# Two transformer layers on one core: index heads in pairs, a wide first block with x split ahead of w, and a norm chunk divided over two groups

## The chip, the cores and the metric

The kernel runs on one core of one Trainium2 chip. Its time is the device time of one execution in microseconds; the median over several executions is given. Engines are named as in the profile: TensorE (PE, with its weight loads as PEld), VectorE (DVE), ScalarE (ACT), GpSimd (POOL) and SyncE (SP), which issues most of the DMAs.

## What is computed

Two layers run one after the other over x of 256 tokens by 2048 (float32). The first layer is a mixer of two attentions, a cross attention to a memory, and a feed-forward part, each followed by a layer norm. The part in which the change lies is the start of the mixer:

```python
proj = x @ w_in
q_dsa, c_kv, q_idx, k_idx, w_idx, q_m, k_m, v_m, ga, gb = split(proj)
c_kv = rms_norm(c_kv, kv_norm_g)
k_idx = layer_norm(k_idx, idx_k_norm_g, idx_k_norm_b)
...
logits = einsum('thd,sd->ths', q_idx, k_idx) * 64 ** -0.5       # 16 index heads of 64
score = einsum('th,ths->ts', w_idx * 16 ** -0.5, relu(logits))  # summed over the heads
score = where(key_pos <= qpos, score, -inf)                     # then the top 64 keys of each query
...
x = layer_norm(ALPHA * x + y, ln_g[0], ln_b[0])                 # the first norm, ahead of the cross attention
```

The second layer (a gated mixer of three attention branches) is not touched.

## The kernel before

**Blocks and groups.** Every projection is cut into blocks of 512 output columns (`NB`), one accumulation for each of the two token tiles (`R = 2`). The contraction over 2048 rows is cut into 16 tiles of 128, taken two at a time (`GK = 2`): one block is 8 groups, and a group is 12 matmuls of 128 x 128 by 512. Twelve, because float32 operands are split into an upper part in the fast format and a rest (x = x_hi + x_lo, w = w_hi + w_lo), and the products hi*hi, hi*lo and lo*hi are summed.

**How a group of weights comes.** SP loads it into one of four slots of `stage` (`group`, L277; it waits until VectorE has finished the group four back, semaphore `lo_done`). ScalarE rounds it to `w_hi` (`split`, L1031, L1043), VectorE subtracts to get `w_lo` (`split`, L1446, L1454), and TensorE's `group` (L542) waits for `lo_done` and multiplies (L552). ScalarE and VectorE run two groups ahead of TensorE (`AHEAD = 2`): their `weights` functions call `split` twice at the first group of a block, once at each of the others but the last, and not at the last. Other work of a stage is put between the groups by hooks: `hook(j)` runs behind group j on every engine. Each engine works through its own list strictly in order.

**The start.** `x` comes in four chunks of 512 columns (`x_chunk`, L297) over SP's queue, the first piece of weights over ScalarE's (L1129). TensorE runs filling turns (`keep_warm`), then turns x by 128 x 128 tiles (`feed_batch`, L590, L594), two batches ahead; ScalarE writes `x_hi` of a batch (`hi_batch`, L1085) and VectorE `x_lo` (`lo_batch`, L1495). Block 1 holds the 256 columns of c_kv and the 80 of k_idx and w_idx (`FIRST_W = 336`), loaded as two pieces per group (256 columns, then 80), and VectorE copies its result out (L1649 to L1656). On ScalarE and VectorE the split of w group 0 stands ahead of the first batch of x. Blocks 2 and 3 are q_idx (512 columns each), 4 and 5 q_dsa, 6 to 9 q and k of the second attention ("qk_m"), 10 and 11 its values. ScalarE copies each of these blocks to `nat` (`to_nat`), TensorE turns it behind group 0 of the next block (`turn`, L571, L577), VectorE copies the turned heads (`heads_in`). The small norms of k_idx and c_kv run on VectorE in the hooks of block 2 (`small_norms`), their results are turned behind group 2 of block 4 (`keys_and_latent`).

**Index heads.** In each of the blocks 6 to 9, behind groups 0, 2, 4 and 6, one of the 16 heads is scored (`index_head`, TensorE L704, ScalarE L1158, VectorE L1717). TensorE multiplies two tiles of queries (128 columns of keys for the first, 256 for the second) into the PSUM bank `AUX`; the head takes 64 of the 128 rows of the array, the lower and the upper half by turns. ScalarE writes the relu to `relu_s`, VectorE adds it, weighted, to `score`. POOL copies the eight tiles of q_idx for the next block after the fourth head.

**The first norm.** The residual is kept in `x_res` (two tiles of 2048 columns). After the last output block, in the block that projects the memory's keys ("K block", weights `w_kv_mem`), VectorE computes the root of the variance behind group 0 (`norm_root`, L1618, which also does the first 256 columns), the next 256 columns behind group 1 (`norm_chunk(0)`) and the 512 columns of the second chunk behind group 2 (`norm_chunk(1)`): `centre` (L1605) and `rescale` (L1614), two instructions each. POOL does the two last chunks at the same time (L494, L500, L505). TensorE turns the finished columns behind groups 5 and 6 and in the next block ("Q block").

```python
            def norm_in(j):

                if j == 0:
                    norm_root(64)
                if 1 <= j <= 2:
                    norm_chunk(j - 1)
                feed_into(x_hi, x_lo, FED_X[0])(j)
```

Of the kernel before, what the change touches and what calls it, by code (L numbers as in the profile page):

```python
# [28 lines left out]
P = 128  # L29
# [115 lines left out]
def two_blocks(nc, a, out, per):  # L145

    ctx = ExitStack()
    with ctx:
# [118 lines left out]
        def width(g):  # L267

            return NB if not isinstance(g, int) or g >= KT // GK else FIRST_W
# [3 lines left out]
        def _(sp):  # L273
# [30 lines left out]
            group(a["w_in"], GK * P, C_LAT, FIRST_W)  # L304
            x_chunk(1)
            group(a["w_in"], 2 * GK * P, C_LAT, FIRST_W)
            group(a["w_in"], 3 * GK * P, C_LAT, FIRST_W)
# [229 lines left out]
        def _(pe):  # L537
# [3 lines left out]

            def group(kt, first, last, hi, lo, n=NB):  # L542
# [17 lines left out]
            def weights(kts=KT, hi=x_hi, lo=x_lo, n=NB, hook=None, before=None):  # L560
                groups = kts // GK
                for j in range(groups):
                    if before:
                        before(j)
                    group(j * GK, j == 0, j == groups - 1, hi, lo, n)
# [114 lines left out]
            feed_weights(x_in, x_landed, n=FIRST_W, warm=lambda: keep_warm(3))  # L680
# [346 lines left out]
        def _(act):  # L1027
# [3 lines left out]
            def split():  # L1031
# [5 lines left out]
                parts = 2 if isinstance(g, int) and (g < KT // GK or G_UV <= g < G_UV + H_DSA * HD // NB) else 1  # L1037
# [91 lines left out]
            for at, width_, to in ((C_LAT, LAT, 0), (C_KIDX, KIDX_W, LAT)):  # L1129
                src = a["w_in"][0:GK * P, ds(at, width_)].rearrange("(t p) n -> p t n", p=P)  # L1130
                act.dma_start(stage[:, 0, :, to:to + width_], src).then_inc(sem("landed0"), 16)
# [16 lines left out]
            for b in range(2):  # L1148
                weights(hook=small_roots if b == 0 else None)
                to_nat()  # L1150
                c.next("tp_done", 2)
            c.next("tp_done", 2)
# [289 lines left out]
        def _(dve):  # L1442
# [198 lines left out]
            split()  # L1641
            for t in range(KT // 2):
                lo_batch(x_hi[:, 2 * t:2 * t + 2, :], x_lo[:, 2 * t:2 * t + 2, :], t)
                if t > 0:
                    split()
                c.next("w_used")
            split()

            for r in range(R):  # L1649
# [7 lines left out]
            split()  # L1657
# [58 lines left out]
            dve.wait_ge(sem("ext"), 32)  # L1716
            def index_head(b, j):  # L1717

                if j % 2:
                    return  # L1720
                dve.wait_ge(sem("idx_read"), c.next("idx_read"))
                for t, (lo, hi) in enumerate(TILE_COLS):
                    ins = dve.scalar_tensor_tensor(
                        out=score[:, lo:hi], in0=relu_s[:, lo:hi],
                        scalar=flat(w_idx[:, t:t + 1, b * 4 + j // 2:b * 4 + j // 2 + 1]),
                        in1=score[:, lo:hi], op0=ALU.mult, op1=ALU.add)
                ins.then_inc(sem("relu_used"), 1)
                dve.wait_ge(sem("relu_used"), c.next("relu_used"))
# [9 lines left out]
            def heads_of(b):  # L1738

                dst, b = (qi_t, b) if b < 2 else (qd_t, b - 2) if b < 4 else (qkm_t, b - 4)  # L1740
                heads_in(lambda t: dst[:, b * 4 + 2 * t:b * 4 + 2 * t + 2, :])

            for b in range(8):
                def q_hook(j):
                    if b > 0 and j == 0:
# [3 lines left out]
                    if b == 0:  # L1749
# [3 lines left out]
                    if b >= 4:  # L1753
                        if j == 0 and b == 4:
                            dve.wait_ge(sem("const"), 1)
                        index_head(b - 4, j)
# [104 lines left out]
            def norm_in(j):  # L1861
# [3 lines left out]
                if 1 <= j <= 2:  # L1865
                    norm_chunk(j - 1)
# [327 lines left out]
```

## Time and profile before

| | us |
|---|---|
| median of 3 runs (lowest, highest) | 2265.49 (2264.25, 2270.46) |
| profiled execution | 2264.81 |
| span in its profile, mean granted clock | 2263.0, 0.996 |
| TensorE busy, instructions | 2240.2, 10253 |
| weight loads (PEld) busy | 1853.4 |
| VectorE busy | 1307.0 |
| ScalarE busy | 1039.1 |
| GpSimd busy | 171.3 |
| DMA: moved, mean rate | 421.28 MB, 186 GB/s |

Matmuls are pipelined: one row of a 512-column matmul shows about 390 ns, while the next one starts 227 ns after it. So rows of the timeline overlap, and the distance between starts is what a matmul costs. In the rows below, "Lnnn" is the line of the kernel; "x12" merges twelve instructions that follow each other.

### The profile page before, as it was taken

The numbers are of one execution on the slowest core, as the hardware profiler recorded it, in microseconds if no ns is written. First come the engines' busy times: TensorE is split into PE (matmuls) and PEld (weight loads), VectorE is DVE, ScalarE is ACT, GpSimd is POOL, SyncE is SP. The second block draws the span as 40 slices with busy tenths as digits, with TensorE's granted clock in tenths as the row PEclk, the third lists the DMA queues.
The fourth block names the chain that finished last, engine by engine and source line by source line (L and its number), as shares of the span: only waits on it lengthen the run. The fifth ranks groups of instructions, "written<-read, shape, count | busy, mean of one in ns | idle before, by whom it ended". The sixth has DMA issues, their size and how long they took to land.

```text
span 2263.0 us, 29600 instructions
## 1 busy us (share of the span) xinstructions
PE 2240.2 (99%) x10253; PEld 1853.4 (82%) x10253; DVE 1307.0 (58%) x1571; ACT 1039.1 (46%) x1239; POOL 171.3 (8%) x175
## 2 busy tenths in 40 slices
PE   8999999999999999999999999999999999999999
PEld 7877888888887788888888888887888888888887
DVE  5555655666667764455445544567565656645674
ACT  4444444555444444433444344435545454445642
POOL 1000000001204130000000000004000000200020
PEclk9999999999999999999999999999999999999999
DMA  7755554656755466656565566554556665665554
GB/s 220 227 166 155 175 163 155 195 154 216 253 187 204 131 206 193 189 192 192 179 200 187 194 190 194 186 186 149 167 176 202 194 195 176 214 186 175 168 190 163
DMA packets 216437, 421.28 MB, mean 186 GB/s; under 512 B 15224, under 2 KB 19360, under 8 KB 214432
## 3 DMA queue, kind: packets, MB, share of 16 engines
q1 hardware_dynamic: 212640, 401.97, 56.7%
q0 software_dynamic: 3168, 17.82, 2.4%
q8 instruction: 55, 0.90, 0.2%
q10 hardware_dynamic: 544, 0.34, 0.1%
q14 instruction: 30, 0.25, 0.0%
HBM read 417.97 MB, written 2.11 MB: 186 GB/s over the span
## 4 chain that ended last, share of the span: by engine, by line
PE 95%; DVE 2%; POOL 1%; DMA 0%; ACT 0%; issue 0%; ACTq 0%; DVEq 0%
PE b_ps L552 89%; PE b_ps L577 1%; PE b_ps L646 1%; PE b_ps L594 1%; DVE b_w_lo L1454 1%; PE b_ps L714 1%; PE b_ps L661 1%; POOL b_x_res L494 1%; DVE b_x_res L1614 0%; DVE b_x_res L1605 0%; PE b_ps L655 0%; DMA b_stage<-in_w_in 0%; PE b_ps L737 0%; POOL b_x_res L505 0%; POOL b_x_res L500 0%
## 5 line engine op out<-in xcount | busy, mean ns | idle before, releaser
L1454 DVE TENSOR_TENSOR b_w_lo<-b_stage,b_w_hi 128x1024 fp32r<-128x1024 f32 (+1 forms) x762 | 934.2, 1245 | 625.4 <-ACT b_w_hi L1043 622.3
L1043 ACT ACTIVATE b_w_hi<-b_stage 128x1024 fp32r<-128x1024 f32 (+1 forms) x762 | 794.4, 1054 | 684.7 <-PE b_ps L552 645.0
L552 PE MATMUL b_ps<-b_w_hi,b_x_hi 128*128 128x512 f32 (+1 forms) x2368 | 942.4, 398 | 4.5 <-DVE b_x_lo L1495 3.9
L552 PE MATMUL b_ps<-b_w_hi,b_x_lo 128*128 128x512 f32 (+1 forms) x2368 | 923.3, 390 | 0.0
L552 PE MATMUL b_ps<-b_w_lo,b_x_hi 128*128 128x512 f32 (+1 forms) x2368 | 922.1, 389 | 0.0
L552 PEld LDWEIGHTS b_ps<-b_w_hi,b_x_hi 128*128 128x128 f32 x2368 | 446.5, 189 | 98.8 <-issue 5.2
L552 PEld LDWEIGHTS b_ps<-b_w_hi,b_x_lo 128*128 128x128 f32 x2368 | 446.2, 188 | 94.1
L552 PEld LDWEIGHTS b_ps<-b_w_lo,b_x_hi 128*128 128x128 f32 x2368 | 446.9, 189 | 87.6
L552 PE MATMUL b_ps<-b_w_hi,b_ff_h 128*128 128x512 f32 x352 | 137.2, 390 | 0.0
L552 PE MATMUL b_ps<-b_w_hi,b_ff_l 128*128 128x512 f32 x352 | 137.0, 389 | 0.0
L552 PE MATMUL b_ps<-b_w_lo,b_ff_h 128*128 128x512 f32 x352 | 136.9, 389 | 0.0
L494 POOL TENSOR_SCALAR b_x_res<-b_x_res,b_mv,b_rstd 128x512 f32<-128x512 f32 x12 | 34.5, 2880 | 871.1 <-DVE b_rstd L1628 871.1
L552 PEld LDWEIGHTS b_ps<-b_w_hi,b_ff_l 128*128 128x128 f32 x352 | 66.1, 188 | 13.9
L552 PEld LDWEIGHTS b_ps<-b_w_hi,b_ff_h 128*128 128x128 f32 x352 | 66.1, 188 | 13.9
L552 PEld LDWEIGHTS b_ps<-b_w_lo,b_ff_h 128*128 128x128 f32 x352 | 66.1, 188 | 13.3
L1593 DVE SCALAR_TENSOR_TENSOR b_x_res<-b_x_res,b_ps 128x512 f32<-128x512 f32 (+1 forms) x48 | 33.0, 688 | 45.5 <-PE b_ps L552 44.9
L1116 ACT ACTIVATE b_logits<-b_logits,b_nmax 128x128 f32<-128x128 f32 (+1 forms) x48 | 21.5, 449 | 80.6 <-DVE b_nmax L1542 80.6
L1085 ACT ACTIVATE b_x_hi<-b_ps 128x512 fp32r<-128x512 f32 x40 | 23.8, 598 | 71.4 <-PE b_ps L594 71.4
L552 PE MATMUL b_ps<-b_w_hi,b_oh 128*128 128x512 f32 x136 | 53.6, 394 | 0.0
L552 PE MATMUL b_ps<-b_w_hi,b_ol 128*128 128x512 f32 x136 | 53.0, 390 | 0.0
L552 PE MATMUL b_ps<-b_w_lo,b_oh 128*128 128x512 f32 x136 | 53.0, 389 | 0.0
L1495 DVE TENSOR_TENSOR b_x_lo<-b_ps,b_x_hi 128x512 fp32r<-128x512 f32 x40 | 27.5, 688 | 30.4 <-ACT b_x_hi L1085 30.4
(286 smaller groups left out, 1461.4 us busy)
## 6 DMA issues: line engine op xcount, KB each, us to landing
b_stage<-in_w_in SPq DMA_DIRECT2D x336, 512.0 KB, 4.1
b_stage<-in_w_ffn_in SPq DMA_DIRECT2D x176, 512.0 KB, 4.5
b_stage<-in_w_ffn_out SPq DMA_DIRECT2D x88, 512.0 KB, 4.2
b_stage<-in_w_out SPq DMA_DIRECT2D x64, 512.0 KB, 4.1
b_stage<-in_w_up SPq DMA_DIRECT2D x24, 512.0 KB, 4.3
b_stage<-in_w_o_dsa SPq DMA_DIRECT2D x16, 512.0 KB, 4.4
b_stage<-in_w_o_moba SPq DMA_DIRECT2D x16, 512.0 KB, 4.5
b_stage<-in_w_kv_mem SPq DMA_DIRECT2D x16, 512.0 KB, 3.6
```

The lines of the kernel that those rows point to most:

```text
L494: pool.tensor_scalar(x, x, mv[:, r, 0:1], rstd[:, r:r + 1], ALU.subtract, ALU.mult)\
L552: ins = mm(ps[:, ACC + r, 0:n], x[:, kt + t, rows], w[:, slot, t, 0:n], start=first and t == 0 and k == 0, stop=last and t == GK - 1 and k ...
L577: ins = T(ps[:, TP + j // 2, (j % 2) * S + r * P:(j % 2) * S + (r + 1) * P], nat[:, r, j * P:(j + 1) * P], ident[:, :])
L594: ins = T(ps[:, TP + t % 2, kk * S + r * P:kk * S + (r + 1) * P], src[:, r, (2 * t + kk) * P:(2 * t + kk + 1) * P], ident[:, :])
L646: ins = mm(ps[:, SC, lo:hi], q[:, t * P:(t + 1) * P], keys(hi - lo), start=k == 0, stop=k == len(pairs) - 1)
L661: mm(ps[:, bank, col:col + S], v0, probs_t[:, 0:S], start=True, stop=False)
L714: ins = mm(ps[:, AUX, lo:hi], qi_st[half, n // 2, t * P:(t + 1) * P], kidx_t[half, 0:hi - lo], start=True, stop=True)
L1043: act.activation(w_hi[:, slot, :, 0:n], stage[:, slot, :, 0:n], ACT.Copy)\
L1085: ins = act.activation(dst, ps[:, TP + t % 2, :].rearrange("p (k s) -> p k s", k=2), ACT.Copy)
L1454: dve.tensor_tensor(w_lo[:, slot, :, 0:n], stage[:, slot, :, 0:n], w_hi[:, slot, :, 0:n].bitcast(F32), ALU.subtract).then_inc(sem("lo_done ...
L1495: ins = dve.tensor_tensor(lo, ps[:, TP + t % 2, :].rearrange("p (k s) -> p k s", k=2), hi.bitcast(F32), ALU.subtract)
L1593: dve.scalar_tensor_tensor(out=x, in0=x, scalar=alpha, in1=ps[:, ACC + r, :], op0=ALU.mult, op1=ALU.add).then_inc(sem(f"tile_out{r}"), 1)
```

## The change

1. *The first block.* Block 1 becomes the first 512 columns of q_idx, with one DMA per group; block 2 is the narrow one (336 columns, two DMAs per group), block 3 the rest of q_idx. On ScalarE and VectorE the first two batches of x are split ahead of w groups 0 and 1. TensorE's very first group has an order of its own (`first_group`): x_hi*w_hi and x_lo*w_hi wait only for `hi`, and x_hi*w_lo comes last, behind the wait for `lo_done`. The result of block 1 goes over `nat` and is turned behind group 0 of block 2; VectorE's copies of the latent stand at the end of block 2, the small norms in block 3.
2. *Index heads in pairs.* Behind groups 0 and 4 two heads follow each other, the first on the lower half of the rows into `AUX`, the second on the upper half into `OT`. ScalarE writes them to `relu_s` and `aux_b`, VectorE adds one after the other. ScalarE's loop over the four blocks is unrolled.
3. *The first norm.* `centre` of the second chunk stays behind group 2, `rescale` goes behind group 3, so that one `split` stands between them.

```diff
-            group(a["w_in"], GK * P, C_LAT, FIRST_W)
+            group(a["w_in"], GK * P, C_QIDX)
             x_chunk(1)
...
             for j in range(4, KT // GK):
-                group(a["w_in"], j * GK * P, C_LAT, FIRST_W)
-            blocks("q_idx", a["w_in"], 0, C_QIDX, 2)
+                group(a["w_in"], j * GK * P, C_QIDX)
+            blockw(a["w_in"], 0, C_LAT, n=FIRST_W)
+            blockw(a["w_in"], 0, C_QIDX + NB)
...
+            def first_group():
+
+                order = ((x_hi, w_hi), (x_lo, w_hi), (x_hi, w_lo))
+                pe.wait_ge(sem("hi"), 1)
+                for k, (x, w) in enumerate(order):
+                    if k == 2:
+                        pe.wait_ge(sem("lo_done"), c.next("lo_done"))
+                    for r in range(R):
+                        for t in range(GK):
+                            ins = mm(ps[:, ACC + r, :], x[:, t, r * P:(r + 1) * P], w[:, 0, t, :],
+                                     start=k == 0 and t == 0, stop=False)
+                ins.then_inc(sem("w_used"), 1)
+                c.next("g")
...
-            feed_weights(x_in, x_landed, n=FIRST_W, warm=lambda: keep_warm(3))
+            feed_weights(x_in, x_landed, warm=lambda: keep_warm(3))
...
-            def index_head(j):
-
-                if j % 2:
+            def index_pair(j):
+
+                if j not in (0, 4):
                     return
-                n = j // 2
-                half = slice((n % 2) * IDX_D, (n % 2 + 1) * IDX_D)
-                if n == 0:
+                if j == 0:
                     pe.wait_ge(sem("qi_staged"), c.next("qi_staged"))
                 pe.wait_ge(sem("idx_read"), c.value("idx_read"))
-                for t, (lo, hi) in enumerate(TILE_COLS):
-                    ins = mm(ps[:, AUX, lo:hi], qi_st[half, n // 2, t * P:(t + 1) * P],
-                             kidx_t[half, 0:hi - lo], start=True, stop=True)
-                ins.then_inc(sem("idx_done"), 1)
-                c.next("idx_read")
-
+                for n, bank in enumerate((AUX, OT)):
+                    half = slice(n * IDX_D, (n + 1) * IDX_D)
+                    for t, (lo, hi) in enumerate(TILE_COLS):
+                        ins = mm(ps[:, bank, lo:hi], qi_st[half, j // 4, t * P:(t + 1) * P],
+                                 kidx_t[half, 0:hi - lo], start=True, stop=True)
+                    ins.then_inc(sem("idx_done"), 1)
+                    c.next("idx_read")
+
+            weights(n=FIRST_W, hook=turn_first())
             weights()
-            weights(hook=turn_first())
             weights(hook=turn_first(keys_and_latent))
             weights(hook=turn_first())
             for b in range(4):
-                weights(hook=turn_first(index_head))
+                weights(hook=turn_first(index_pair))
...
-            split()
             for t in range(KT // 2):
                 hi_batch(x_hi[:, 2 * t:2 * t + 2, :], t)
-                if t > 0:
+                for _ in range((0, 2)[t] if t < 2 else 1):
                     split()
                 c.next("w_used")
             for _ in range(AHEAD):
                 split()
+            to_nat()
+
+            weights()
             skip_block()
+            c.next("tp_done", 2)
...
-            with c.loop(act, "qk_m", 4):
-                def index_head(j):
-                    if j % 2 == 0:
-                        act.wait_ge(sem("idx_done"), c.next("idx_done"))
-                        act.wait_ge(sem("relu_used"), c.value("relu_used"))
-                        act.activation(relu_s[:, :], ps[:, AUX, 0:CW], ACT.Relu).then_inc(sem("idx_read"), 1)
-                        c.next("relu_used")
-                weights(hook=index_head)
+            for _ in range(4):
+                def index_pair(j):
+                    if j in (0, 4):
+                        for dst, bank in ((relu_s[:, :], AUX), (aux_b[:, 0:CW], OT)):
+                            act.wait_ge(sem("idx_done"), c.next("idx_done"))
+                            if c.value("relu_used", 1) > 0:
+                                act.wait_ge(sem("relu_used"), c.value("relu_used", 1))
+                            act.activation(dst, ps[:, bank, 0:CW], ACT.Relu).then_inc(sem("idx_read"), 1)
+                            c.next("relu_used")
+                weights(hook=index_pair)
...
-                if 1 <= j <= 2:
-                    norm_chunk(j - 1)
+                elif j == 1:
+                    norm_chunk(0)
+                elif j == 2:
+                    centre(slice(NB, 2 * NB))
+                elif j == 3:
+                    rescale(slice(NB, 2 * NB))
                 feed_into(x_hi, x_lo, FED_X[0])(j)
```

## Rows read from the trace of the kernel before

**Rows 1.** The page, part 1: busy time, share of the span, instructions of TensorE.
```profile
PE 2240.2 (99%) x10253; PEld 1853.4 (82%) x10253; DVE 1307.0 (58%) x1571; ACT 1039.1 (46%) x1239; POOL 171.3 (8%) x175
```

**Rows 2.** TensorE's waits, whole span: us in total, times, longest us.
```profile
PE b_ps L552 <- DVE b_x_lo L1495: 3.9, 1, 3.9
PE b_ps L552 <- DVE b_w_lo L1454: 2.4, 2, 2.2
```

**Rows 3.** DMA issues from ScalarE's queue, 0 to 60 us: size, us to landing.
```profile
b_stage<-in_w_in ACTq DMA_DIRECT2D x1, 256.0 KB, 5.2
...
b_stage<-in_w_in ACTq DMA_DIRECT2D x1, 80.0 KB, 7.6
```

**Rows 4.** Stretches: us, busy per engine, then PEclk (granted clock), DMA share, GB/s.
```profile
5.00:6.00 1.00, 0.00 (x0) 0.00 (x0) 0.00 (x0) 0.00 (x0) 0.70 (x4) 1.00 1.05 347
...
12.00:13.00 1.00, 1.00 (x6) 1.00 (x5) 0.72 (x1) 0.00 (x0) 0.00 (x0) 0.50 1.08 381
```

**Rows 5.** Timeline, blocks 1 and 4: start, duration, engine, line, operation, idle before.
```profile
6.10 1.06 PE L594 MATMUL b_ps<-b_ident,b_gate_a 128*128 128x128 f32 x8 [1.16 <-DMA b_gate_a<-in_x]
...
9.77 1.07 ACT L1085 ACTIVATE b_x_hi<-b_ps 128x512 fp32r<-128x512 f32 x2
...
14.88 0.60 PE L594 MATMUL b_ps<-b_ident,b_gate_a 128*128 128x128 f32 x4
...
15.51 0.60 ACT L1085 ACTIVATE b_x_hi<-b_ps 128x512 fp32r<-128x512 f32 x1 [4.02 <-PE b_ps L594]
...
79.00 1.03 PE L577 MATMUL b_ps<-b_ident,b_nat 128*128 128x128 f32 x8
```

**Rows 6.** The splits in 0 to 60 us, wide and narrow: ns min/median/max, forms.
```profile
L1043 ACT ACTIVATE b_w_hi<-b_stage x21: 756/1051/1062, 9.1 to 56.6; 128x1024 fp32r<-128x1024 f32 x13, 128x672 fp32r<-128x672 f32 x8
L1454 DVE TENSOR_TENSOR b_w_lo<-b_stage,b_w_hi x21: 849/1219/1228, 9.9 to 58.9; 128x1024 fp32r<-128x1024 f32 x13, 128x672 fp32r<-128x672 f32 x8
```

**Rows 7.** The chain in order of time, blocks 1 to 3: start us, us, what.
```profile
11.41 3.63 PE b_ps L552 x12
...
15.47 1.84 PE b_ps L552 x12
...
17.80 2.08 PE b_ps L552 x12
...
57.35 21.81 PE b_ps L552 x96
```

**Rows 8.** The same chain at the index heads (L714).
```profile
126.18 0.85 PE b_ps L714 x4
...
133.58 5.67 PE b_ps L552 x24
139.25 0.85 PE b_ps L714 x4
```

**Rows 9.** Idle time of the weight loads ahead of the heads: us, times, longest.
```profile
PEld b_ps L714 <- issue: 4.9, 16, 0.4
```

**Rows 10.** The chain at the scores of a MoBA head (L646, 128 rows).
```profile
465.22 0.66 PE b_ps L646 x4
465.87 5.47 PE b_ps L552 x24
```

**Rows 11.** Timeline of the first norm, VectorE and TensorE.
```profile
687.64 3.48 DVE L1605 SCALAR_TENSOR_TENSOR b_x_res<-b_x_res,b_mv,b_vec_a 128x512 f32<-128x512 f32 x2
691.05 3.45 DVE L1614 SCALAR_TENSOR_TENSOR b_x_res<-b_x_res,b_rstd,b_vec_b 128x512 f32<-128x512 f32 x2
...
703.51 4.19 DVE L1454 TENSOR_TENSOR b_w_lo<-b_stage,b_w_hi 128x1024 fp32r<-128x1024 f32 x2 [2.53 <-ACT b_w_hi L1043]
...
692.86 0.60 PE L594 MATMUL b_ps<-b_ident,b_x_res 128*128 128x128 f32 x4
695.69 0.50 PE L552 MATMUL b_ps<-b_w_hi,b_mem_hi 128*128 128x512 f32 x1 [2.24 <-DVE b_w_lo L1454]
...
698.55 0.60 PE L594 MATMUL b_ps<-b_ident,b_x_res 128*128 128x128 f32 x4
```

More of the change, by code:

```diff
@@ L267, in width @@
         def width(g):
-            return NB if not isinstance(g, int) or g >= KT // GK else FIRST_W
+            return FIRST_W if isinstance(g, int) and 1 <= g // (KT // GK) < 2 else NB
         @block.sync
@@ L303, in _ @@
             c.next("g")
-            group(a["w_in"], GK * P, C_LAT, FIRST_W)
+            group(a["w_in"], GK * P, C_QIDX)
             x_chunk(1)
-            group(a["w_in"], 2 * GK * P, C_LAT, FIRST_W)
-            group(a["w_in"], 3 * GK * P, C_LAT, FIRST_W)
+            group(a["w_in"], 2 * GK * P, C_QIDX)
+            group(a["w_in"], 3 * GK * P, C_QIDX)
             x_chunk(2)
@@ L564, in weights @@
                         before(j)
-                    group(j * GK, j == 0, j == groups - 1, hi, lo, n)
+                    if isinstance(c.value("g"), int) and c.value("g") == 0:
+                        first_group()
+                    else:
+                        group(j * GK, j == 0, j == groups - 1, hi, lo, n)
                     if hook:
@@ L1036, in split @@
                 slot = (c.base.get("hi", 0) + c.local.get("hi", 0)) % SLOTS
-                parts = 2 if isinstance(g, int) and (g < KT // GK or G_UV <= g < G_UV + H_DSA * HD // NB) else 1
+                parts = 2 if isinstance(g, int) and (width(g) == FIRST_W or G_UV <= g < G_UV + H_DSA * HD // NB) else 1
                 act.wait_ge(sem(f"landed{slot}"), c.next(f"landed{slot}", 16 * parts))
@@ L1127, in out_hi @@
                 act.activation(dst, ps[:, OT, 0:S], ACT.Copy).then_inc(sem("oh_done"), 1)
-            for at, width_, to in ((C_LAT, LAT, 0), (C_KIDX, KIDX_W, LAT)):
-                src = a["w_in"][0:GK * P, ds(at, width_)].rearrange("(t p) n -> p t n", p=P)
-                act.dma_start(stage[:, 0, :, to:to + width_], src).then_inc(sem("landed0"), 16)
+            src = a["w_in"][0:GK * P, C_QIDX:C_QIDX + NB].rearrange("(t p) n -> p t n", p=P)
+            act.dma_start(stage[:, 0, :, :], src).then_inc(sem("landed0"), 16)
             for name in TOKENS["act"]:
                 act.nop().then_inc(sem(name), 1)
-            split()
             for t in range(KT // 2):
                 hi_batch(x_hi[:, 2 * t:2 * t + 2, :], t)
-                if t > 0:
+                for _ in range((0, 2)[t] if t < 2 else 1):
                     split()
@@ L1147, in small_roots @@
                     root(sd[:, 0:R])
[L1148 to L1152, printed above, removed]
+            weights(hook=small_roots)
+            to_nat()
+            c.next("tp_done", 2 + 2)
             for b in range(2):
@@ L1639, in _, with heads_of @@
                 dve.nop().then_inc(sem(name), 1)
-            split()
             for t in range(KT // 2):
                 lo_batch(x_hi[:, 2 * t:2 * t + 2, :], x_lo[:, 2 * t:2 * t + 2, :], t)
-                if t > 0:
+                for _ in range((0, 2)[t] if t < 2 else 1):
                     split()
                 c.next("w_used")
-            split()
+            skip_block()
+            for _ in range(AHEAD):
+                split()
+            dve.wait_ge(sem("ext"), 32)
+            def heads_of(b):
+                dst, b = (qi_t, b) if b < 2 else (qd_t, b - 2) if b < 4 else (qkm_t, b - 4)
+                heads_in(lambda t: dst[:, b * 4 + 2 * t:b * 4 + 2 * t + 2, :])
+            weights(hook=lambda j: heads_of(0) if j == 0 else None)
             for r in range(R):
@@ L1656, in _ @@
                 c.next(f"tile_out{r}")
-            split()
             def var_of(x, n, mean, eps):
@@ L1715, in small_norms, with index_pair @@
                     latent_normed()
-            dve.wait_ge(sem("ext"), 32)
-            def index_head(b, j):
-                if j % 2:
+            def index_pair(b, j):
+                if j not in (0, 4):
                     return
[L1721 to L1728, printed above, removed]
+                for n, relu in enumerate((relu_s, aux_b)):
+                    h = b * 4 + j // 2 + n
+                    dve.wait_ge(sem("idx_read"), c.next("idx_read"))
+                    for t, (lo, hi) in enumerate(TILE_COLS):
+                        ins = dve.scalar_tensor_tensor(
+                            out=score[:, lo:hi], in0=relu[:, lo:hi],
+                            scalar=flat(w_idx[:, t:t + 1, h:h + 1]),
+                            in1=score[:, lo:hi], op0=ALU.mult, op1=ALU.add)
+                    ins.then_inc(sem("relu_used"), 1)
+                    dve.wait_ge(sem("relu_used"), c.next("relu_used"))
             def keys_and_latent():
@@ L1736, in keys_and_latent @@
                 c.next("tp_free", 2)
[L1738 to L1743, printed above, removed]
+            for b in range(1, 8):
                 def q_hook(j):
-                    if b > 0 and j == 0:
+                    if b > 1 and j == 0:
                         heads_of(b - 1)
```

4 lines of the change are left out of this document (2 added, 2 removed).

## The prediction

> **What bounds the kernel now.** I read the page first (TensorE's row), then its waits over the whole run, then the chain in order of time and the timeline in the three stretches that the diff touches. TensorE is busy for 2240.2 of 2263.0 us [rows 1]. Of the 22.8 us without work, one wait of 3.9 us for the first x_lo and two of together 2.4 us for w_lo lie in the touched stretches [rows 2]. So every microsecond that TensorE works or waits less, at whatever stage, comes off the end. VectorE, ScalarE and the DMAs count only where they make TensorE wait or run slowly. The change is therefore summed as TensorE's time in three places.
>
> **Place 1, the first three blocks of w_in.** Before, block 1 is the narrow one (336 columns) and two wide ones (512) follow; after, the order is wide, narrow, wide. The work is the same, so what counts is when TensorE starts, at which clock, and how long it stalls. I carry a clock from the first weight matmul to the turn behind group 0 of block 4, which is the same point of the work in both kernels and stands at 79.00 now [rows 5].
>
> *The start.* Now group 0 waits for its second, narrow piece: 256 KB land after 5.2 us, the 80 KB (rows of 320 bytes) only after 7.6 us [rows 3]. ScalarE then splits w and after it x, and TensorE starts at 11.41 [rows 7], though x chunk 0 had been turned from 6.10 on [rows 5]. After, w of group 0 is one piece of 512 KB with rows of 2 KB. The queues move 347 GB/s around then, with the DMA engines full [rows 4]; x chunk 0 and this piece are together 1 MB, against 768 KB that land by 6.1 now, so both should land 0.25 MB / 347 GB/s = 0.7 us later, near 6.8. The turns start there, x_hi follows 0.63 us after the start of a turn (14.88 to 15.51) and two of them take 1.07 [rows 5]; w_hi takes 1.05 in wide form and 0.76 in narrow [rows 6]: 6.8 + 0.63 + 1.07 + 1.05 = 9.55. The new first group needs only w_hi for its first 8 matmuls, which is 1.8 us of work (5.47 us for 24 [rows 10]), and w_lo comes 1.2 us behind w_hi, so that wait is hidden. As a bound, w lands at 9.08 as now: start at 10.2.
>
> *The clock.* The granted clock was 1.00 in 5 to 6 us, inside the idle time of 1.16 us ahead of 6.10 [rows 4, 5], and 0.50 in 12 to 13 us, after 3.9 idle us; group 0 took 3.63 us where the next took 1.84 [rows 4, 7]. After, TensorE is idle from about 8.2 (the end of the turns and the three filling ones) to 9.55, 1.35 us. That is nearer to the first, so I take the full clock. If it falls all the same, 12 wide matmuls take twice their 2.73 us: 2.7 us.
>
> *The blocks.* A wide group takes 2.86 us when a turn stands ahead of it (695.69 to 698.55 [rows 11]), a turn 0.35. The chain from a turn to the group that needs it is now 14.88 to 17.80 = 2.92 us [rows 5, 7]; wide splits add (1.05 - 0.76) + (1.22 - 0.85) = 0.66 [rows 6]: 3.58, against turn, group and turn on TensorE, 3.56. It stays balanced, but the last group has one turn less ahead of it and waits 0.4. Block 1 ends at 9.55 + 6 x 3.2 + 2.86 + 0.4 + 2.86 = 34.9. Block 2 is 8 x 1.84 [rows 7], the turn that moved into it (0.79) and 0.1 for its restart: 50.5. Block 3 is 21.8 [rows 7]: 72.3. Group 0 of block 4, 2.7: 75.0, which is 4.0 us ahead of 79.00. I take 0.2 off for waits in the balanced chain: **-3.8 us** (late landing and fallen clock together: -0.4).
>
> *What is moved with it.* VectorE's copies of the latent move to the end of block 2, ahead of a wide group as before; the small norms move to block 3 and are read in block 4 behind group 2, some 10 us after they end. ScalarE's evacuation of q_idx now stands ahead of a narrow group: its second tile takes 0.65 us from the end of block 1, and the half group that needs the bank starts 0.92 us after it. SP issues as many DMAs as before. SP's and ScalarE's unrolled loops have no row of their own; TensorE and VectorE run these blocks unrolled now and show no wait, so 0.
>
> **Place 2, the index heads.** A head stands alone between groups: 0.85 us, and the two groups behind it take 5.67 [rows 8]. The same shape on all 128 rows, a MoBA head, costs 0.66 with 5.47 behind it [rows 10]. So 0.39 us of each head are the step to 64 rows and back. The weight loads show where: they sat idle ahead of each of the 16 heads, 4.9 us in all [rows 9]. After, two heads share one step: 8 x 0.39 = **-3.1 us**. Bounds: 0, if the way from one half of the rows to the other costs as much; beyond 3.1, if the halves overlap (below). The second piece of ScalarE (0.5 us) and of VectorE (0.75) at j = 0 and 4 stands ahead of the next split on their queues, but TensorE reads that split only after two more groups, 5.5 us: no cost. POOL copies the next q_idx two groups earlier, free.
>
> **Place 3, the first norm.** Between two splits VectorE centres for 3.48 us and rescales for 3.45, with POOL at work beside it. TensorE turns at 692.86 and starts its group only at 695.69 instead of 693.2 [rows 11]: 2.5 us lost. After, the split of this group comes behind the centring, at 691.1 + 1.2 = 692.3, in time. Rescaling runs to 695.7, the next split to 697.0; its group could start at 693.2 + 2.86 + 0.35 = 696.4 and waits 0.6. What follows is a chain over ScalarE's evacuation at the block's end and two splits of 2.1 us from 703.51 [rows 11]; it starts with the end of that block and moves along. Sum: **-1.9 us** (bounds -0.5, if POOL makes the late split later still, and -2.5).
>
> **Sum.** -3.8 - 3.1 - 1.9 = -8.8 us. The profiled execution took 2264.8 us (span 2263.0 and 1.8 around it), 0.7 below the median of three, 2265.5: 2256.0 for such an execution, 2256.7 for the median.
>
> **The rivals.**
> - *One gain fails.* The clock falls in group 0 (-2.7 of gain), or w lands late, or place 1's new start is swallowed by ScalarE's order, or a pair drains between its halves (-3.1), or the norm gives half. For it: none of these was seen in the new form, and the clock rests on an idle time 0.2 us shorter. About 3 us less: 2259.7. With two failed: 2262.5.
> - *The halves overlap.* The last pass of a pair's first head (256 columns) and the passes of the second head's short matmul lie on different rows and write different banks. A MoBA head streams 768 columns in 0.66 us [rows 10], so 256 are 0.22 us; hidden once per pair they are 8 x 0.22 = 1.8 us more: 2254.9. Against: no row has two halves back to back. The Trainium skill, TensorEngine Tiling (Array Packing), section Tiling Modes, says that a change of the tiling mode drains TensorE and a change of tile doesn't, and that different tiles can load and multiply in parallel; by it both the 3.1 and the 1.8 us come. No run yet shows the second.
> - *The narrow block starves: slower.* Block 2 wants 336 KB, in two pieces, per 1.84 us; the same groups come every 2.3 to 2.6 us now. A slot's way is landing, w_hi 0.76 and w_lo 0.85 [rows 6]. With 4 slots TensorE begins to wait once (landing + 1.6) / 4 is over 1.84, from a landing of 5.8 us, and six groups pay. At 11.7 us the gain of 8.8 is gone; at 13.5 us it is 6 x 1.94 = 11.6 us of loss: 2268.3. For it: the 80 KB took 7.6 us [rows 3]. Against: that was beside x chunks in full queues; one of 7.6 costs 6 x 0.46 = 2.8 at most, and the first slots of block 2 are requested long ahead, behind wide groups.
>
> **How the numbers follow.** Forecast as summed 0.45; halves overlap 0.18; one gain fails 0.27; two or more fail 0.07; starving, slower 0.03. To hold 8 in 10 the range goes from 2253.8 (overlap, and the norm at its bound) to 2261.0 (one failed and half of another). A difference under 0.3%, 6.8 us, can't be told from no change; that line is at 2258.7. Faster: 0.45 + 0.18, less 0.05 for sizes that come out small, and a fourth of the third case: 0.65. Slower by over 0.3% needs a landing near 16 us or a stall not seen here: 0.02. The rest, 0.33, is same.
>
> **What the profile after would show.** Place 1: the first weight matmul near 9.6 us, released by w_hi, with a granted clock of 1.00 in 9 to 13 us, and the turn in block 4 near 75.0. Place 2: 8 idle times of the weight loads instead of 16, and four groups with their heads in 12.6 to 12.7 us, instead of 126.18 to 139.25 [rows 8], 13.1. Place 3: no wait for w_lo over 1 us in the first norm. It would be wrong with a clock of 0.50 in the first wide group, with 13.1 us for a pair and its groups, with TensorE waiting in block 2 while ScalarE waits for stage, or with a wait behind the rescaling as long as the old one.

## The result and the profile after

| | before | after |
|---|---|---|
| median (lowest to highest), us | 2266.22 (2264.25 to 2270.46), 4 runs | 2253.77 (2252.45 to 2254.82), 4 runs |
| profiled execution, its span, us | 2264.81, 2263.0 | 2252.45, 2250.6 |
| TensorE busy, us | 2240.2 | 2231.8 |
| ratio, 95% interval | | 0.9942 [0.9925, 0.9960] |

The kernel became 12.45 us faster (0.55%), where 8.8 were forecast. The time lies 0.03 us below the range, whose lower end was 2253.8. The direction was right and the size was not. Two of the sum's three terms were a little too large (by 1.1 and 0.4 us) and one was far too small (by 5.4 to 5.7), so that errors in part cancelled. That the time fell just outside the range and not just inside is chance: the same kernel, measured again below, gave 2254.17. The median of the kernel before had also been 0.7 us lower when the forecast of 2256.7 was made from it.

I took the sum apart at fixed points of the work, which both chains pass. First the kernel before (the chain in order of time: start us, us, what): the turn in block 4, a point shortly before the first norm, and the first turn behind the norm's next block.

```profile
79.16 0.87 PE b_ps L577 x8
...
673.94 1.41 PE b_ps L552 x6
...
724.20 0.87 PE b_ps L577 x8
```

The same chain of the kernel after, from the start on:

```profile
6.44 0.65 PE b_ps L612 x4
...
7.11 1.09 ACT b_x_hi L1103 x2
8.19 0.95 ACT b_w_hi L1061
...
9.28 4.34 PE b_ps L552 x12
...
33.12 4.89 PE b_ps L567 x24
...
76.44 0.87 PE b_ps L595 x8
...
123.45 0.86 PE b_ps L732 x8
124.31 11.14 PE b_ps L567 x48
135.46 0.86 PE b_ps L732 x8
...
662.44 1.41 PE b_ps L567 x6
...
711.20 0.87 PE b_ps L595 x8
```

The turn in block 4 comes at 76.44 instead of 79.16: place 1 gave 2.7 us. The point ahead of the norm comes 11.50 earlier (673.94 to 662.44), so 8.8 lie between, and the index heads are all that was changed there. The turn behind the norm comes 13.00 earlier (724.20 to 711.20): place 3 gave 1.5. At the end of the span 12.4 are left; the 0.6 us between are not assigned to any part. This last stretch took 1538.8 to 1539.3 us in the four profiled executions without all three parts, and 1539.4 to 1541.0 in the eight with them, so a few tenths may come with the change; no run separates that.

*Place 1.* TensorE started at 9.28, released by ScalarE's w_hi and 2.1 us before the 11.41 of [rows 7], but its first group of 12 took 4.34 us instead of 2.8. The stretches say why (us, busy per engine, PEclk, DMA share, GB/s): the granted clock fell to 0.50, which is 1.2 of 2.4 GHz, although TensorE had been idle for only 1.45 us. That clock was one of the signs that the prediction had named as speaking against it.

```profile
9.00:10.00 1.00, 0.72 (x2) 0.66 (x3) 0.86 (x2) 0.13 (x1) 0.94 (x3) 0.50 0.66 250
...
12.00:13.00 1.00, 1.00 (x6) 0.81 (x4) 0.84 (x1) 0.00 (x0) 0.00 (x0) 0.93 1.05 406
```

*Place 2.* A pair of heads takes 0.86 us, as long as a single head did [rows 8]. Two heads and the four groups around them went from 13.07 us [rows 8] to 12.01 (123.45 to 135.46). The weight loads sat idle 8 times instead of the 16 of [rows 9]:

```profile
PEld b_ps L732 <- issue: 2.1, 8, 0.4
```

ScalarE, which copies the two heads out, finds the second one ready when it is through with the first: no idle time stands in the row of `b_aux_b` (timeline: start, duration, engine, line, operation, idle time before).

```profile
124.34 0.49 ACT L1182 ACTIVATE b_relu_s<-b_ps 128x384 f32<-128x384 f32 x1 [1.95 <-PE b_ps L732]
124.72 0.49 ACT L1182 ACTIVATE b_aux_b<-b_ps 128x384 f32<-128x384 f32 x1
```

*Place 3.* The wait of 2.24 us of [rows 11] is gone; what is left of it is 0.47 us, one group later. Rows of the timeline, of VectorE, of GpSimd beside it, and of that group:

```profile
676.15 3.48 DVE L1625 SCALAR_TENSOR_TENSOR b_x_res<-b_x_res,b_mv,b_vec_a 128x512 f32<-128x512 f32 x2
679.55 2.31 DVE L1474 TENSOR_TENSOR b_w_lo<-b_stage,b_w_hi 128x1024 fp32r<-128x1024 f32 x1
681.79 2.44 DVE L1634 SCALAR_TENSOR_TENSOR b_x_res<-b_x_res,b_rstd,b_vec_b 128x512 f32<-128x512 f32 x2
...
675.70 3.38 POOL L501 TENSOR_TENSOR b_x_res<-b_x_res,b_vec_a 128x512 f32<-128x512 f32 x2
679.05 3.96 POOL L506 TENSOR_TENSOR b_x_res<-b_x_res,b_vec_b 128x512 f32<-128x512 f32 x2
...
685.84 0.50 PE L567 MATMUL b_ps<-b_w_hi,b_mem_hi 128*128 128x512 f32 x1 [0.47 <-DVE b_w_lo L1474]
```

The split between the two halves of the norm took 2.31 us, not the 1.2 that I had put down, and the rescaling behind it took 2.44, not 3.45. In the chain, centring, rescaling and a split take 7.9 us before and 8.0 after. Which of them is slow depends on what GpSimd does at that time. Beside its TENSOR_TENSOR instructions (L501 and L506; 675.70 to 683.0 here, and again from 688.84 on) a split takes 2.1 to 2.3 us. Beside its TENSOR_SCALAR (L495) splits take 1.15 to 1.6, and 1.2 without GpSimd. The Trainium skill, GPSIMD Engine Reference, section Specifications, has GpSimd's SBUF interface shared with VectorE, with contention for VectorE's instructions with two SBUF inputs; the split and the norm's instructions both read two tensors there, and these rows agree. VectorE's x_lo, which takes one of its two inputs from PSUM, keeps its 0.68 us in this stretch.

### The profile page after: what moved, and what is told of

It reads as the page before. It is cut to its first block, busy times and chain, and to the rows that moved or that the text cites. A ratio compares the mean times of both kernels' runs of the same rounds, so it can differ in the third digit from the quotient of the medians.

```text
span 2250.6 us, 29502 instructions
## 1 busy us (share of the span) xinstructions
PE 2231.8 (99%) x10253; PEld 1849.3 (82%) x10253; DVE 1307.6 (58%) x1571; ACT 1038.5 (46%) x1239; POOL 171.6 (8%) x175
## 4 chain that ended last, share of the span: by engine, by line
PE 95%; DVE 2%; POOL 1%; ACT 0%; issue 0%; DMA 0%; ACTq 0%; DVEq 0%
PE b_ps L567 90%; PE b_ps L595 1%; PE b_ps L664 1%; PE b_ps L612 1%; DVE b_w_lo L1474 1%; PE b_ps L679 1%; POOL b_x_res L495 1%; DVE b_x_res L1625 0%; DVE b_x_res L1634 0%; PE b_ps L673 0%; PE b_ps L755 0%; PE b_ps L732 0%; POOL b_x_res L506 0%; POOL b_x_res L501 0%; PE b_ps L680 0%
## 5 line engine op out<-in xcount | busy, mean ns | idle before, releaser
L495 POOL TENSOR_SCALAR b_x_res<-b_x_res,b_mv,b_rstd 128x512 f32<-128x512 f32 x12 | 33.7, 2811 | 869.3 <-DVE b_rstd L1648 869.3
```

The source lines that it names most:

```text
L495: pool.tensor_scalar(x, x, mv[:, r, 0:1], rstd[:, r:r + 1], ALU.subtract, ALU.mult)\
```

## The experiments

The theory at this point had three parts: the heads gained from overlap, not from the saved step alone; the start was earlier but lost 1.5 us to the clock; the norm gained 1.5. The first four runs take the parts alone, and forbid the overlap.

**Pairs alone.** The kernel before with `index_pair` on TensorE, ScalarE and VectorE; start and norm as before.

```diff
...
-                weights(hook=turn_first(index_head))
+                weights(hook=turn_first(index_pair))
...
```

> The kernel before, with the index heads in pairs and nothing else. In the changed kernel's chain a pair took 0.86 us with 11.12 for the four groups behind it, against 2 x (0.85 + 5.67) before: 1.06 us per pair, 8.5 in all. Theory A (the pairs are worth this by themselves): -8.5 us against before. Rival (part of it comes from the new first block, which moves the small norms and slots): clearly less than 8.5 here, about the 3.1 to 4.9 of the prediction.

Measured: 2258.19 us (2257.73 to 2260.80), ratio 0.9965 [0.9953, 0.9978], that is 7.9 us less than before (5.0 to 10.7). The chain shows the pair as in the kernel after, 12.01 us from pair to pair:

```profile
79.46 0.87 PE b_ps L577 x8
...
126.47 0.86 PE b_ps L714 x8
127.33 11.14 PE b_ps L552 x48
138.48 0.86 PE b_ps L714 x8
...
665.46 1.41 PE b_ps L552 x6
```

From the turn in block 4 to the point ahead of the norm it is 586.00 us here, exactly as in the kernel after, and 594.78 in the kernel before. So the pairs alone bring the 8.8 us, 8.5 in their own blocks and 0.3 behind them, and the rival (a part comes from the new first block) is refuted. They are some two thirds of the whole gain. The rest of this trace shows something else: at the undivided norm the clock fell behind the wait of 2.2 us, and the group there took 4.27 us, where it took 3.02 in the kernel before.

```profile
686.00:688.00 2.00, 0.78 (x3) 0.67 (x4) 2.00 (x3) 0.56 (x1) 2.00 (x1) 1.00 0.00 0
...
690.00:692.00 2.00, 2.00 (x9) 1.60 (x7) 1.91 (x2) 0.00 (x0) 2.00 (x2) 0.50 0.87 275
```

**The first block alone.** The kernel after with the heads and the norm as before.

```diff
-                weights(hook=turn_first(index_pair))
+                weights(hook=turn_first(index_head))
...
-                elif j == 2:
-                    centre(slice(NB, 2 * NB))
-                elif j == 3:
-                    rescale(slice(NB, 2 * NB))
+                if 1 <= j <= 2:
+                    norm_chunk(j - 1)
```

> The kernel before, with the new first block alone (wide, x ahead of w, first_group). The chain says that the turn in block 4 comes at 76.3 instead of 79.0: -2.7 us, if nothing behind gives it back. The prediction said -3.8. The clock should fall again just before or in the first group.

Measured: 2265.28 us (2263.32 to 2268.10), ratio 0.9994 [0.9985, 1.0004]: 1.4 us less, which can't be told from none. Its trace has the turn in block 4 at 78.00, so 1.2 us were there at that point; The expectation of 76.3 was missed: the eight turns of x took 1.94 us here (1.07 in the kernel after), TensorE started at 9.98 and its first group took 4.90. The clock then fell at the norm's wait here too.

```profile
78.00 0.87 PE b_ps L595 x8
...
695.76 4.61 PE b_ps L567 x12
```

The starving rival had no chance to show itself: the narrow block's pieces landed in at most 4.1 us, here and in the kernel after, below the 5.8 at which I had put the start of waiting, and TensorE didn't wait in block 2. The slow landings of this trace, up to 6.5 us, are those of block 3's wide pieces. By them VectorE comes late to the copies at the end of block 2, and TensorE waits 0.3 us for these.

**The norm alone.** The kernel before with `centre` behind group 2 and `rescale` behind group 3.

```diff
-                if 1 <= j <= 2:
-                    norm_chunk(j - 1)
+                elif j == 1:
+                    norm_chunk(0)
+                elif j == 2:
+                    centre(slice(NB, 2 * NB))
+                elif j == 3:
+                    rescale(slice(NB, 2 * NB))
```

> The kernel before, with the divided norm chunk alone. By the chain of the changed kernel -1.5 us (forecast -1.9); if VectorE and POOL only fall differently beside each other, within half a microsecond of before.

Measured: 2264.25 us (2263.60 to 2270.10), ratio 0.9992 [0.9982, 1.0001]: 1.8 us less, which can't be told from none by the time alone. In the chain the way from the turn in block 4 to the turn behind the norm is 643.50 us here (79.66 to 723.16) and 645.04 in the kernel before (79.16 to 724.20): 1.5 us, the same as in the kernel after.

```profile
79.66 0.87 PE b_ps L577 x8
...
691.57 2.23 DVE b_w_lo L1454
...
723.16 1.09 PE b_ps L577 x8
```

**Both heads on the same half.** The kernel after, where both heads of a pair read the lower 64 rows, so that half of the scores are computed from the wrong head; the count and the size of the instructions are the same, and only the rows of the array differ.

```diff
-                    half = slice(n * IDX_D, (n + 1) * IDX_D)
+                    half = slice(0, IDX_D)
```

> The changed kernel with both heads of a pair on the lower half of the rows; the second head of each pair is computed from the first one's queries, so half of the index scores are left out of the output. Theory A (both halves work side by side from the first matmul on): a pair costs 0.85 + 0.66 = 1.5 us instead of 0.86, +5.2 us in all against the changed kernel, and only the saved step of 3.1 is left of the 8.5. Rival (a second head is cheap once the array is in the 64-row mode, whatever its rows): no difference.

Measured: 2260.53 us in its one run, 8.1 more than the kernel after in its profiled execution. The chain of waits has 1.50 us for the pair instead of 0.86, and the groups behind it unchanged; ScalarE waits 0.17 us more for the second head, behind the copy of the first.

```profile
123.86 1.50 PE b_ps L732 x8
125.37 11.11 PE b_ps L567 x48
```

ScalarE's row for the second head (timeline):

```profile
125.41 0.49 ACT L1182 ACTIVATE b_aux_b<-b_ps 128x384 f32<-128x384 f32 x1 [0.17 <-PE b_ps L732]
```

This settles Place 2, and the rival with it. The second head costs 0.64 us on the same half and nothing on the other: 8 x 0.64 = 5.1 us of overlap. What is left of the 1.06 per pair is the saved step to 64 rows and back: 0.85 + 0.85 + 2 x 5.67 before against 1.50 + 11.11, that is 0.43 per pair and 3.4 us in all. The other 3.0 us of this run's distance lie outside the heads: 0.4 ahead of them (the turn in front of the first pair ends at 123.86 instead of 123.45), the rest in later waits, one of them of 0.67 us. It is one execution, and I take from it only the heads.

The next two runs ask whether the findings can be used: one step for four heads, and a start that keeps its clock. Two more undo the parts of the new start one at a time. None of these four has the kernel after measured beside it; their ratios are to the kernel before, and the intervals overlap with that of the kernel after. So I read them by their traces.

**Four heads in one place.** The kernel after, with all four heads of a block behind group 0, in four banks.

```diff
-                if j not in (0, 4):
+                if j != 0:
                     return
...
-                for n, bank in enumerate((AUX, OT)):
-                    half = slice(n * IDX_D, (n + 1) * IDX_D)
+                for n, bank in enumerate((AUX, OT, SC, PT)):
+                    half = slice((n % 2) * IDX_D, (n % 2 + 1) * IDX_D)
...
-                        ins = mm(ps[:, bank, lo:hi], qi_st[half, j // 4, t * P:(t + 1) * P],
+                        ins = mm(ps[:, bank, lo:hi], qi_st[half, n // 2, t * P:(t + 1) * P],
...
```

> The changed kernel with all four heads of a block behind group 0, in four PSUM banks: two rounds of a lower and an upper half. If halves overlap fully and only heads on the same rows follow each other, a quad costs 0.86 + 0.64 = 1.5 us and needs one step to 64 rows, against two pairs with two steps (2 x (0.86 + 0.2)) now: 0.6 us per block, -2.4 us against the changed kernel. Rival (VectorE, with four heads to add behind group 0, gives the split of group 4 late): TensorE waits in blocks 6 to 9 and nothing is won.

Measured: 2251.41 us (2250.29 to 2251.99), ratio 0.9932 [0.9915, 0.9948].

```profile
121.72 0.87 PE b_ps L595 x8
122.59 1.61 PE b_ps L731 x16
124.21 22.01 PE b_ps L567 x96
146.22 0.87 PE b_ps L595 x8
```

A block with its heads takes 24.50 us instead of 24.86 (122.58 to 147.44 in the kernel after): 0.36 per block, 1.4 in all, for one step less. This is a second measurement of the step, beside the 0.43 above, if two pairs directly behind each other cost what they cost apart; the 0.39 of the prediction lies between them. Four heads cost 1.61 us together, less than two times 0.86. The expectation of 0.6 per block had left out the 0.2 us that the quad's own step costs behind it: 2 x 1.06 less 1.7 is 0.4. TensorE didn't wait in these blocks, so the rival with VectorE is refuted.

**More filling matmuls.** The kernel after with 20 and 8 filling turns instead of 15 and 3.

```diff
-            keep_warm(15)
-            feed_weights(x_in, x_landed, warm=lambda: keep_warm(3))
+            keep_warm(20)
+            feed_weights(x_in, x_landed, warm=lambda: keep_warm(8))
```

> The changed kernel with 20 filling turns ahead of x (15 now) and 8 behind the first turns (3 now), so that TensorE is hardly idle before the first group. If the idle time before the first group is what makes its clock fall, the first group takes 2.8 us instead of 4.3 and the median falls by 1 to 1.5 us. Rival (the clock in the first 15 us does not follow these short idle times): the first group is slow in some executions as before, and the time stays within 0.5 us.

Measured: 2252.02 us (2251.87 to 2252.04), ratio 0.9933 [0.9917, 0.9950]. Its four runs lie within 0.17 us. The first four matmuls took 1.16 us at a granted clock of 1.00; in the kernel after they took 2.05. The turn in block 4 came at 75.65.

```profile
9.11 1.16 PE L552 MATMUL b_ps<-b_w_hi,b_x_hi 128*128 128x512 f32 x4 [0.90 <-ACT b_w_hi L1061]
```

And its chain behind that:

```profile
10.60 1.07 ACT b_w_hi L1061
...
11.70 1.24 DVE b_w_lo L1474
...
13.07 3.01 PE b_ps L567 x12
...
75.65 0.87 PE b_ps L595 x8
```

With the clock kept, the second group waits 0.47 us, because its weights landed only at 10.58. So the fallen clock cost not its whole 1.5 us but 0.8 (76.44 to 75.65), less than the 1 to 1.5 us expected. Nor does one need the filling for a fast first group: the run with four heads has the old filling, the same 1.45 us without work, and 1.15 us for its first four matmuls. Its turn in block 4 came at 75.58. In the run with both heads on the same half, again with 1.45 us without work, the clock fell as in the kernel after (2.04 us for the four).

```profile
9.26 1.15 PE L552 MATMUL b_ps<-b_w_hi,b_x_hi 128*128 128x512 f32 x4 [1.45 <-ACT b_w_hi L1060]
```

**The first group in the ordinary order.** The kernel after without `first_group`, so that group 0 waits for w_lo.

```diff
-                    if isinstance(c.value("g"), int) and c.value("g") == 0:
-                        first_group()
-                    else:
-                        group(j * GK, j == 0, j == groups - 1, hi, lo, n)
+                    group(j * GK, j == 0, j == groups - 1, hi, lo, n)
```

> The changed kernel without first_group: the first group waits for w_lo like every other. w_lo of group 0 came 1.25 us behind w_hi, so the first matmul comes 1.2 us later and the turn in block 4 too: +1.2 us, at the same clock. Rival (the DMA or ScalarE sets group 1 anyway, so the early start is given back): no difference at that turn.

Measured: 2257.08 us (one run). TensorE started at 10.60 instead of 9.28 and its first group took 5.36 us; the turn in block 4 came at 78.94, 2.5 us later than in the kernel after. The later start is 1.3 of it, as expected; the rest is the clock, which was not: 0.50 from 9 to 15 us, behind 2.71 us without work. The group in the chain, and the last full stretch at the low clock:

```profile
10.60 5.36 PE b_ps L567 x12
```

```profile
14.00:15.00 1.00, 1.00 (x4) 0.71 (x3) 0.00 (x0) 0.00 (x0) 0.00 (x0) 0.50 1.05 383
```

**w ahead of x.** The kernel after, where ScalarE and VectorE split w group 0 ahead of the first batch of x.

```diff
+                if t == 0:
+                    split()
                 hi_batch(x_hi[:, 2 * t:2 * t + 2, :], t)
-                for _ in range((0, 2)[t] if t < 2 else 1):
+                if t > 0:
                     split()
...
```

> The changed kernel with w of group 0 split ahead of x, on ScalarE and VectorE, as before the change. w landed at 6.6 us in the changed kernel, before the turns were done: w_hi would end at 7.7, x_hi at 8.3, w_lo at 8.9, x_lo at 9.6, so a start 0.3 to 0.6 us later than 9.28. Then the one-piece load, not the order of the splits, brought most of the earlier start. Rival (the order is what brought it): a start near 11 us.

Measured: 2254.84 us (one run). TensorE started at 9.65, released by x_lo. That is 0.4 later than in the kernel after, as expected, and still 1.8 ahead of 11.41 [rows 7]. So of the 2.1 us by which TensorE starts earlier, the order of x and w carries 0.4; the order inside the first group, which need not wait for w_lo, carries 1.3 by the run before this one; and the weights in one piece were there at 6.67, where the narrow piece had landed at 9.08. These shares don't add up to 2.1 exactly, since each part hides some of the others. Two things limit them. In the two other traces with the old start (pairs alone, norm alone) the narrow piece landed at 8.2 and TensorE started at 10.6, so the 2.1 us were 1.3 there. And the 0.4 hold only where the turns are fast: this run's turns took 1.94 us, and the two traces with x ahead of w and such slow turns start at 9.98 and 10.06, later than the 9.65 here.

```profile
0.94 5.73 DMA b_stage<-in_w_in
...
9.00 0.61 DVE b_x_lo L1517
...
9.65 4.94 PE b_ps L552 x12
```

**Again, and both.** The kernel after ran once more, unchanged, beside a version with the four heads in one place and the 20 and 8 filling turns.

> The changed kernel itself, unchanged, for one more execution of its start beside the others. If the clock in its first group is a matter of the execution: either the group takes 2.8 us with the turn in block 4 at 75.6, or 4.3 us with the turn at 76.4, and its times spread over at least that 0.8 us. If it is a matter of the 1.45 idle us ahead of the group: 4.3 us and 76.4 again, and times about 0.8 us above the version with more filling at the same heads.

Measured: 2254.17 us (2251.66 to 2256.57), ratio 0.9943 [0.9929, 0.9956]. This execution was neither of the two expected ones. The eight turns took 1.94 us instead of 1.07, TensorE started at 10.06, its first four matmuls took 2.04, and the turn in block 4 came at 77.18. Through all of this the record of the granted clock says 1.00. Rows of the timeline:

```profile
6.40 1.94 PE L612 MATMUL b_ps<-b_ident,b_gate_a 128*128 128x128 f32 x8 [1.21 <-DMA b_gate_a<-in_x]
...
10.06 2.04 PE L552 MATMUL b_ps<-b_w_hi,b_x_hi 128*128 128x512 f32 x4 [1.08 <-ACT b_w_hi L1061]
```

and of the stretches:

```profile
10.00:11.00 1.00, 0.94 (x2) 0.83 (x3) 1.00 (x1) 0.19 (x1) 0.11 (x1) 1.00 1.05 408
```

So the start of one and the same kernel differs by 0.7 us between two executions (76.44, 77.18), and the same program's times spread over 4.9 us.

> The changed kernel with both steps that helped it alone: the four heads of a block in one place (0.37 us less per block from turn to turn, 1.5 in all) and more filling matmuls ahead of the first group, 20 and 8 instead of 15 and 3 (first four matmuls in 1.16 us instead of the slow ones). If the two are independent: first group at 9.1 to 9.3 us at full clock, turn in block 4 at 75.6, blocks of 24.5 us with their heads, and a time of 2250.5 to 2251.5. If the filling only moved luck about: within 0.5 us of the changed kernel's own time in the same call.

Measured: 2250.69 us (2250.25 to 2252.34), ratio 0.9927 [0.9914, 0.9941], a time as expected. It has the lowest median here, 3.5 us below the kernel after measured beside it (2254.17; the two spreads touch at 2251.66 to 2252.34) and 16.4 below the kernel before. From the run with four heads alone (2251.41) it can't be told. TensorE started at 9.83, later than the 9.1 to 9.3 expected, behind eight turns of 1.71 us; its first group took 3.00, at the full clock, the turn in block 4 came at 75.71, and a block with its heads took 24.50.

## Why the prediction was wrong

*Place 2: the term that failed.* The sum had 8 x 0.39 = 3.1 us for the saved step and nothing for an overlap of the two heads. The step was right: 3.4 by one comparison, 0.36 a block by the other. The overlap, 5.1 us, failed twice. I put it among the rivals, on the ground that no row has two halves back to back; and even there I let only the last pass of the first head (256 columns) meet the second, 0.22 us per pair. Measured are 0.64, the whole second head: the group behind a pair starts as early as behind one head (0.86 and 0.85). A second head's own price could have been bounded by rows. Of the 0.39 only 0.19 lie in the head itself (0.85 against 0.66), the other 0.20 in the groups behind it (5.67 against 5.47) [rows 8, 10]; a second head is then 0.66 us, and "all of it" 8 x 0.66 = 5.3 us instead of 1.8. The range would have reached 2251.4. As it stood its lower end didn't even follow from its own terms: overlap, and the norm at its bound, give 2254.3 and not 2253.8. The Trainium skill, TensorEngine Tiling (Array Packing), section Tiling Modes, says both that a change of mode drains TensorE and that different tiles load and multiply in parallel. The traces agree with both, as far as times can: 0.36 to 0.43 us for the one, 0.64 for the other. I had weighed its second sentence too lightly and sized it by an order of passes that no row showed.

*Place 1: right mechanism, smaller size.* Forecast 3.8 us, measured 2.7. The start was right: 9.28 against 9.55, released by w_hi, as worked out. The clock was the step that failed: 1.35 idle us were taken as too few for it to fall; 1.45 were enough in this execution. The price that I gave, 2.7 us for the whole group at 1.2 GHz, was too high for it (the run in the ordinary order paid nearly that, 5.36 us for its group), since the clock was back before its last third: the group took 1.5 us longer than 2.8, and 0.3 of that was won back by the earlier start. I also missed the second group: its weights landed at 10.58 in the run with a fast first group, so that a perfect first group gives only 0.8 of the 1.5. By the terms of the prediction: block 1 was to end at 34.9; group 7 starts at 33.12 here, and with 2.86 for it the block ended at 36.0, which is the 1.1 missing. From there to the turn in block 4 it was 40.5 us, forecast 40.1; 0.16 of the difference is that I compared a sum of the chain with the timeline's 79.00, where the chain has 79.16. No wait stood in block 2; the landings at which the starving rival begins never came, so it stays untested. The 2.7 is also one execution's outcome. The same start put this turn at 75.58 in one trace and at 78.00 in another, against 79.16 to 79.66 in the three with the old start: 1.2 to 4.1 us, and with the full clock nearly the forecast.

*Place 3: right, 0.4 too much.* Forecast 1.9, measured 1.5, twice. The step that failed is the split's time behind the centring: 1.2 taken from undisturbed rows, 2.31 beside GpSimd. So w_lo came just too late and not in time, and its group started 0.56 us after the turn instead of 0.35 (681.36 to 681.92). At the next group the 0.6 us that I had expected were 0.7 (684.77 to 685.84, less 0.35), of which the trace shows 0.47 as idle: 2.5 - 0.2 - 0.7 is 1.6. Beyond the sum, the traces with the undivided norm show a fallen clock behind its 2.2 us wait in two of three executions (4.27 and 4.61 us instead of 3.02), and none of the nine executions with the divided norm does. By the turn behind the norm both had lost 1.3 us against the kernel before. So the division also takes away a loss of 1.3 us that the kernel before seems to have in some executions. The profile of before happened to be one without it. That this is why the times of the kernel before spread more (6.2 us in the first comparison, against 2.4 after) is only argued: the later runs of the kernel after spread over 4.9.

*The parts together.* 2.7 + 8.5 + 1.5 = 12.7, with 0.3 more behind the heads, which came with the pairs alone too, and 0.6 lost later: 12.4 of span. The single versions gave 7.9, 1.4 and 1.8 (from ratios whose intervals reach 2 to 3 us to either side), together 11.1; the changed kernel's ratio gives 13.1. The difference is within these intervals; the fallen clock at the norm, seen in two of the three, would be a cause for it, which is not shown.

*What stays open.* Why the same program begins with turns of 1.07 us in one execution and of 1.94 in another, I can't say. The slow ones were seen with either start, in five of the twelve profiled executions, and a sixth changed from slow to fast in the middle (1.71 us). Whether more filling turns keep the clock isn't settled either: both traces with 20 and 8 of them have a fast first group, but so has one with 15 and 3. The four times within 0.17 us speak for it, the five of the last version, 2.1 us apart, don't.

## What to carry to other kernels

Where small matmuls use half of TensorE's rows, put two of them, one on each half, directly behind each other: the second was free here (0.86 us for the pair, 0.85 for one), and the pair paid the step to half the rows and back only once. Price a rival by its full bound, not by the part of it for which a mechanism can be drawn. Where an instruction is moved beside GpSimd's work, take its duration from a row with GpSimd at work; and where a wait lies near the length at which the clock has been seen to fall, put the fallen clock into the range, since one profile shows only one of the two outcomes.

## What the hardware showed unexpectedly

- Two heads on different halves of the rows took no longer than one, although the program has them one after the other: 0.86 us for both, 1.50 on one half, 1.61 for four on two halves.
- TensorE's clock fell to 1.2 GHz behind 1.45 idle us in two executions and stayed at 2.4 behind the same 1.45 us in another (2.05, 2.04 and 1.15 us for the same four matmuls).
- In the first 15 us the record of the granted clock can say 1.00 while the matmuls run at half speed (1.94 us for eight turns, otherwise 1.07).
- VectorE's centring, rescaling and split took 7.9 and 8.0 us in the two orders beside GpSimd, but the split went from 1.15 us behind GpSimd's TENSOR_TENSOR instructions to 2.23 beside them, and the rescaling from 3.38 to 2.37 (in the chain).
